# Two tiles of squares instead of four in the layer norms, and GpSimd's sums for the second half placed between output blocks

## The reference, cut to what matters

```python
def _layer_norm(x, g, b):
    mu = jnp.mean(x, -1); var = jnp.mean(jnp.square(x - mu), -1)
    return (x - mu) * lax.rsqrt(var + LN_EPS) * g + b
h = _layer_norm(ALPHA * h + mix, g, b)
```

## Time and profile before

| | us |
|---|---|
| median of 3 runs | 2943.66 |
| the profiled execution, its own time | 2939.69 |
| its span in the trace | 2937.9 |
| TensorE matmul busy | 2776.6 (95%) |
| VectorE busy | 1276.4 (43%) |
| ScalarE busy | 1030.3 (35%) |
| GpSimd busy | 303.4 (10%) |

### The profile page before, as it was taken

One profiled execution on the slowest core, in us unless ns is written; L12 is line 12 of the kernel. 1 busy time (PEld: TensorE's weight loads), 2 busy tenths in 40 slices (PEclk: granted clock), 3 DMA queues, 4 the chain that ended last, 5 costly groups with the idle time before them and its releaser, 6 DMA issues.

```text
span 2937.9 us, 39976 instructions
## 1 busy us (share of the span) xinstructions
PE 2776.6 (95%) x16594; PEld 2415.9 (82%) x16594; DVE 1276.4 (43%) x2132; ACT 1030.3 (35%) x1624; POOL 303.4 (10%) x357
## 2 busy tenths in 40 slices
PE   8888999999999999999999999997988889999997
PEld 6777899999978879788888888887866687888886
DVE  4444553333422323463334533336566744533333
ACT  4544343222322223352222422224465533422221
POOL 0000210000200000220001200014122230300002
PEclk9999999999999999999999999998999999999998
DMA  3101233222111212232222232221311212232220
GB/s 132 44 30 58 80 107 103 87 94 80 44 55 61 86 58 79 87 101 93 93 96 77 108 100 94 93 79 58 115 51 51 80 50 66 83 116 95 94 65 29
DMA packets 66533, 232.88 MB, mean 79 GB/s; under 512 B 8880, under 2 KB 9264, under 8 KB 65968
## 3 DMA queue, kind: packets, MB, share of 16 engines
q1 hardware_dynamic: 66352, 230.31, 23.7%
HBM read 228.15 MB, written 2.10 MB: 78 GB/s over the span
## 4 chain that ended last, share of the span: by engine, by line
PE 83%; DVE 6%; ACT 5%; POOL 3%; issue 3%; SPq 0%; DMA 0%; DVEq 0%; POOLq 0%; ACTq 0%
PE ps L540 72%; PE ps L837 2%; POOL R L2418 2%; PE ps L560 2%; PE ps L550 1%; PE ps L715 1%; PE ps L676 1%; PE ps L824 1%; POOL S L2407 1%; DVE HT L1759 1%; PE ps L571 1%; ACT HT L1143 1%; DVE XL L1749 1%; DVE SCR L2239 1%; DVE HT L1739 1%
## 5 line engine op out<-in xcount | busy, mean ns | idle before, releaser
L540 PE MATMUL ps<-XH,WH 128*128 128x264 f32 (+2 forms) x1856 | 545.8, 336 | 12.4 <-DVE XL L2381 7.7
L540 PE MATMUL ps<-XH,LENT 128*128 128x512 f32 (+2 forms) x2096 | 526.1, 344 | 7.5 <-DVE XL L1749 7.5
L540 PE MATMUL ps<-XL,WH 128*128 128x264 f32 (+2 forms) x1856 | 530.6, 328 | 0.0
L540 PE MATMUL ps<-XH,WL 128*128 128x264 f32 (+2 forms) x1856 | 529.2, 328 | 0.0
L540 PE MATMUL ps<-HH,LENT 128*128 128x264 f32 (+2 forms) x2220 | 494.2, 320 | 7.4 <-DVE HL L1719 7.4
L1712 DVE TENSOR_TENSOR WL<-RAW,WH 128x1024 fp32r<-128x1024 f32 (+1 forms) x232 | 286.6, 1236 | 289.6 <-ACT WH L1113 289.1
L540 PEld LDWEIGHTS ps<-XH,LENT 128*128 128x128 f32 x2096 | 357.7, 191 | 58.1 <-DVE XL L1749 10.7
L540 PEld LDWEIGHTS ps<-HH,LENT 128*128 128x128 f32 x2220 | 363.8, 191 | 37.6 <-issue 7.6
L540 PEld LDWEIGHTS ps<-XH,WH 128*128 128x128 f32 x1856 | 326.7, 194 | 50.4 <-POOL SCR L2443 7.7
L540 PEld LDWEIGHTS ps<-XH,WL 128*128 128x128 f32 x1856 | 325.2, 193 | 28.7
L540 PEld LDWEIGHTS ps<-XL,WH 128*128 128x128 f32 x1856 | 325.1, 193 | 26.5
(11 more groups left out here) (223 smaller groups left out, 2794.7 us busy)
## 6 DMA issues: line engine op xcount, KB each, us to landing
RAW<-in_wf SPq DMA_DIRECT2D x128, 512.0 KB, 3.3
RAW<-in_wr SPq DMA_DIRECT2D x48, 512.0 KB, 3.3
RAW<-in_wg SPq DMA_DIRECT2D x44, 512.0 KB, 3.2
RAW<-in_wu SPq DMA_DIRECT2D x44, 512.0 KB, 3.3
RAW<-in_wd SPq DMA_DIRECT2D x32, 512.0 KB, 3.2
RAW<-in_we SPq DMA_DIRECT2D x24, 512.0 KB, 3.8
RAW<-in_wm SPq DMA_DIRECT2D x24, 512.0 KB, 3.3
RAW<-in_wro SPq DMA_DIRECT2D x16, 512.0 KB, 3.3
```

The source lines that it names most:

```text
L540: mm = e.matmul(o[:, at:at + m], wt, xt[:, k, c0 + a * m:c0 + (a + 1) * m], start=(n == 0 and j == 0), stop=(n == nk - 1 and j == 2))
```

## The change

```diff
 # TensorE
-            pump(3)
-            ht = [HT[:, i, 0:T] for i in (1, 2, 3, 4)]
-            rstd((ln, half), [(ht[0], S.add_pool[(ln, half, 4)]), (ht[1], S.add_dve[(ln, half, 6)]),
-                              (ht[2], S.sq[(ln, half, 6)]), (ht[3], S.sq[(ln, half, 7)])],
+            pump(5)
+            rstd((ln, half), [(HT[:, 1, 0:T], S.add_pool[(ln, half, 4)]), (HT[:, 2, 0:T], S.add_dve[(ln, half, 7)])],
                  T, (S.normed, ln, half, 7), pump, 3)
 # ScalarE, squares
                 if k == 7:
-                    w.wait_ge(*S.add_dve[ln, half, 4])
+                    w.wait_ge(*S.add_dve[ln, half, 3])
 # ScalarE, output steps
-                pump(1)
+                pump(2)
 # VectorE
+            def add_square(k):
+                w.wait_ge(*S.sq[ln, half, k])
+                if k > 3:
+                    w.wait_ge(*S.add_dve[ln, half, {5: 3, 6: 5, 7: 6}[k]])
+                e.tensor_tensor(HT[:, 2, 0:T], HT[:, 2, 0:T], HT[:, SQ_SLOT[k], 0:T],
+                                ALU.add).then_inc(*S.add_dve(ln, half, k))
 ...
                 if k in (4, 6):
-                    (wait for the square of k - 1, and add it to HT[2])
+                    add_square(k - 1)
                 pump(1)
+            add_square(6)
+            add_square(7)
 # VectorE, output steps
-                pump(1)
+                pump(2)
 # GpSimd
-        def layer_norm(ln, half, T, res, dst):
+        def layer_norm(ln, half, T, res, dst, between={}):
             (adds of the squares 2 and 4, as before)
+            for m in between.get(-1, ()):
+                sums(*m)
             for k in range(8):
                 (new R of block k, as before)
+                for m in between.get(k, ()):
+                    sums(*m)
 ...
+            def ends(half):
+                return [(name, base + m, m, c0 + half * T // 2, T // 2, half) for m in range(8 - n_end, 8)]
+            for m in ends(0):
+                sums(*m)
+            second = ends(1)
+            between = {-1: second[0:2], 0: second[2:3], 3: second[3:4], 6: second[4:5]}
             for half in (0, 1):
-                for m in range(8 - n_end, 8):
-                    sums(name, base + m, m, c, T // 2, half)
-                layer_norm(ln, half, T // 2, lambda k: R[:, k, c:c + T // 2], dst)
+                layer_norm(ln, half, T // 2, lambda k: R[:, k, c:c + T // 2], dst, {} if half else between)
```

## The result

The changed kernel took 2982.04 us, the median of four runs (2978.09 to 2989.87), against 2943.44 before (also of four, the three of the first section among them): a ratio of 1.0129 (95% interval 1.0102 to 1.0156). It is slower, as forecast, but by 38.6 us where 22.7 were forecast; 2982 lies above the range of 2947 to 2974.

A forecast was written before the change was run, and what follows sets the result against it. TensorE, busy 95% of the span, was taken as the bound, delays at second-half `total` or last XL lost one for one. Terms 4.8 + 15.4 + 0.7 - 1.2 + 3.0 = +22.7 us gave 2965 us, range 2947 to 2974.

The forecast's parts named there:

- The squares: Every half norm, last square to root: one VectorE add, four matmuls and three handovers take 1.1 us, 0.3 us more.
- Two steps beside each output step: Second halves: a further split and eviction move ahead of the last XL; +15.4 us including 0.3 six times for squares.
- The clock: Second halves of ln10, ln11, ln3: longer TensorE waits make the low clock likely at the resume; +3 us, 0 to 7.
- GpSimd's sums: First halves: sums between output blocks make `total` 0.9 us later in five norms, +0.3 in ln00; +4.8 us in all.
- block 7's wait of 1.4: First halves: GpSimd's block 7 waits for XL 6, the last residual and the sum behind block 6; 1.4 us.
- The two sums behind the adds of squares: First halves, GpSimd: two sums beside VectorE's last centrings and adds cost the chain 0.8 us, bounds 0 and 1.6.
- ln1: First half +2.8 us, second half -2.8 as its panel copy comes earlier; with 0.3 and mem's 0.4, +0.7 us.
- ln4: `total` follows three sums and seven blocks, -0.7 us; fewer one-column matmuls at low clock, -0.5; together -1.2 us.
- Mem: The squares' price in mem, taken as +0.4 us and counted in the ln1 term.
- the early sums: Rival, at second-half `total`: TensorE finds S1 ready and its 18.7 us wait shrinks; about -12 us net, 2932; chance 0.08.
- absorbed: Rival, second half: extra splits and evictions fall into VectorE's waits for GpSimd; only +6 us, 2950; chance 0.12.
- everything collides: Rival: full port blocking, and low clock between sum of squares and spread in first halves; +10, 2975 us; chance 0.12.

The follow-up runs named there:

- keep_busy: Six useless matmuls of ones on TensorE while it waits for the last add of squares, against the changed kernel; 2974.93 us, ratio 1.0114 to before.
- third_sum_last: Changed kernel with adds ahead of the eviction, one second-half fill step; against that, GpSimd's third sum behind block 7, not 6; 2945.37 us, ratio 1.0008 to before.
- the squares alone: Kernel before with only the change's two tiles of squares and its five fill steps ahead of the sum of squares; 2967.17 us, ratio 1.0071.
- the sums alone: Kernel before with GpSimd's second-half sums between output blocks and two fill steps beside output steps in the first half only; 2949.27 us, ratio 1.0011.
- bare_outputs: Kernel before with no fill step beside the second half's output steps (two in ln1); 2930.19 us, ratio 0.9964.

## Why the prediction was right in direction and too small

*The squares (0.3 us a half norm): the step that failed.* The text worked the price from the last square on: one add, four matmuls, three handovers. That is what it costs where VectorE is free at that moment (0.35 us in ln11's first half). It listed which fill steps moved beside the output steps, but did not place the new adds in VectorE's own order. Step 17 was evicted between the last centring and the root before too (root at 8.97 in ln10's second half against 7.18 in its first); the sum of squares then did not need VectorE any more. The new adds made it wait. In the four second halves that made the stretches 11.9 us longer, measured alone, where 1.2 was forecast: 7.3 us at the roots, the rest behind them, with the low clock.

*Two steps beside each output step (13.6 us without the squares, 13.2 of it in the four): right mechanism, too small.* Split 2.1 and eviction 1.1 to 1.4 are what was measured between two XL; the first eviction, moved from output step 1 to 0, cost about half a us more. With that XL 7 came 4.1 to 4.3 us later, not 3.1 to 3.5, 16.9 us together, and 24.2 us were lost in the four stretches: the other 7.3 stand behind XL 7, where the forecast had only the 3 us of the next paragraph.

*The clock (3 us): too small.* The text read one low window, of ln1, and expected one more fall in each of three norms. In the changed kernel it falls twice in each of ln00, ln10, ln11 and ln3, behind the squares and behind the last XL. The mean granted clock is 0.971 before, 0.965 after and 0.969 in keep_busy. With its two levels of 1.00 and 0.50 that makes some 170 us of the span at the low one before and some 209 after (an estimate from these means and the spans). What of it is lost cannot be told exactly, since a part falls beside waits; 5.9 us are what filling one of the two spells gave back in the four stretches.

*GpSimd's sums (+4.8 us in the first halves): right mechanism, somewhat small.* +6.6 in the change, +5.2 alone, where 4.8 less the squares' 1.8 leaves 3.0. ln00 took +1.3 instead of 0.3. XL 7 came 3.6 to 4.0 us later in the five others where 4.0 was said, and block 7's wait of 1.4 is what third_sum_last gave back in the mean. The two sums behind the adds of squares: the root of ln11's first half came 1.09 us later, 0.35 of it by the squares alone and 0.73 by the sums alone; 0.3 and 0.8 were said.

These 0.73 us do not speak against the Trainium skill's exclusive lock (SBUF — State Buffer, "SBUF: two separate sides"). The 1.6 us that the prediction worked out by it came of charging each sum to the chain in full length, not of the rule. GpSimd and VectorE in ln11's first half with the sums alone:

```profile
1614.32 1.77 POOL L2407 TENSOR_TENSOR S<-S,R 128x256 f32<-128x256 f32 x2
...
1614.57 0.41 DVE L1777 TENSOR_TENSOR R<-ps,R 128x256 f32<-128x256 f32 x1
1614.90 0.61 DVE L1733 TENSOR_TENSOR R<-R,HT 128x256 f32<-128x256 f32 x1
1615.44 0.94 DVE L1739 TENSOR_TENSOR HT<-HT 128x256 f32<-128x256 f32 x1
```

The operation that reads PSUM is not slowed (0.41 us). The two that read two SBUF tiles are, by 0.2 and 0.5 us beside the usual 0.42, and the second one ends 0.29 us behind the sums: it looks held until the sum was through. The same shape is in the earlier trace rows, where VectorE's centring of 0.96 us ends 0.27 us behind GpSimd's two adds. So for these forms the trace agrees with a lock held for whole instructions; the price was small since only two of VectorE's operations with two SBUF inputs met the sums. The sum of the prediction went by the measured rows, and so it loses nothing by this.

*ln1 (+0.7) and ln4 (-1.2):* +0.5 with mem, and -0.9 (ln4's halves -0.40 and -0.46). ln4 held. ln1 came out by luck. Its first half took +3.65 where 2.8 was said, but for the squares' reason, with the root 4.2 us later behind a residual and a split; the sums alone gave +0.95 there. Mem took +1.15 instead of 0.4, and ln1's second half gave back 4.3 instead of 2.8.

*The rivals:* the early sums did not pay, nothing was absorbed; the result lies beyond "everything collides". The low clock between squares and spread, which that rival put into the first halves, came in the second halves; the adds behind the eviction were in no rival.

## What to carry to other kernels

When an operation is added to a chain, write down what stands ahead of it on its own engine at that place; an eviction that was harmless between two chain operations is not harmless once a third stands behind it. Work moved "beside" a step is moved ahead of the next step: put none where it paces TensorE's last dependency (bare_outputs won 1.2 to 3.2 us a norm by that). Fill behind the root, where VectorE waits anyway, cost nothing that the runs show. Where TensorE must stand for some us, reckon what follows at the low clock too.

## What the runs showed of the hardware that was not expected

Six useless matmuls (twelve records, 1.58 us) in what was a wait of 2.97 us kept the granted clock at 1.00 in the four us behind ln11's root, where it was 0.50 without them. A VectorE operation with two SBUF inputs took 0.61 to 0.96 us instead of 0.42 when it started while GpSimd added two SBUF tiles; the residual, with one input in PSUM, took 0.41 beside the same sums. What makes the two long stretches differ by up to 10 us between profiled executions stays open.
